# A hybrid trunk layer with expert retrieval: 128 tokens sent ahead of the other 384, dense expert stages cut from 384 to 256 tokens

## Chip, cores and metric

The kernel runs on one core of one Trainium2 chip. The metric is the device time of one execution in microseconds (us), from launch to the last output. All data are float32, and every weight is read from device memory during the execution.

## The reference

```python
def reference(x, p, ...):                     # x: 512 tokens x 1024, one layer
    h = rms_norm(x, mix_norm)
    aq, ak, av, rq, rk, rv, rg, ga, gr = split(h @ w_in)      # 9216 columns
    y_att = sliding_window_gqa(rope(aq), rope(ak), av, sinks) @ w_o_att   # 8 heads of 128, window 128
    yr = group_norm(retention(rope(rq), rope(rk), rv)) * silu(rg)         # 4 heads, keys 256, values 512
    x = x + (sigmoid(ga) * y_att + sigmoid(gr) * (yr @ w_o_ret)) @ w_out
    x = x + peer(rms_norm(x, ffn_norm))
    x = x + sigmoid(rms_norm(x, ple_norm) @ w_ple_gate) * (p @ w_ple_proj)
    return rms_norm(x, final_norm)

def peer(h):                                   # 8 heads, 16384 experts of one neuron
    q = h @ w_peer_query                       # 2048 columns: 8 heads x 2 halves x 128
    s1, s2 = scores of both halves with 128 sub-keys each
    top 16 of s1, top 16 of s2, top 16 of their 256 sums -> 128 experts a token, softmax gates
    act = gelu(h . expert_down[idx]);  return sum(act * gate * expert_up[idx])
```

Retention is computed as one causal product with a decay matrix over all 512 tokens.

## The kernel before, in words

**Layout.** Activations lie transposed: 8 tiles (`KT`) of 128 features, with tokens along the free dimension. Weights come as units of 128 x 1024 floats (512 KB) in the order of `weight_units`, 390 of them, through a ring of 8 slots (`RING`) filled by SyncE's queue. A slot is loaded again when the unit 8 before has been used (`wait_used`).

**Precision.** Every large product is made of three matmuls of the rounded type float32r (`mm3`: high x high, high x low, low x high). ScalarE writes the high part of a unit (`upper`, L550), GpSimd the low part (`lower`, L493). Small products (scores, transposes, the scatter below) are plain float32 matmuls; the profile records each of these as two.

**Stages, in TensorE's order.** All 512 tokens pass each stage together.
1. Projections and mixers (`columns`: weights stationary, 512 tokens moving; `tokens`: 128 tokens stationary, 512 columns moving; retention heads `for i in range(RH)`, then attention heads `for i in range(AH + 4)`, then `woa`, `ga`, `out`).
2. Queries: 16 units `pq`, each followed by `key_scores`. VectorE then finds the top 16 lists (`best`), decodes positions into expert numbers (`rows_and_columns`, `decode`) and makes the gates.
3. Dense experts for the first 384 tokens (`TD`). `down`: 128 units (keys), each 24 passes over `TZ` = 352 tokens, then gelu on ScalarE, results written to `act_scratch`. From turn 8 on (a turn is 8 units) the gates are scattered into dense form: VectorE makes one-hots (`compare`, `times_gate`), TensorE multiplies them (`scatter`, L1185, 96 groups of four), ScalarE stages them, and they are written to `gate_scratch`. `up`: 128 units, each 18 passes of 512 columns over three token tiles; activations and gates are read back by quads of units (`read_back`), multiplied by VectorE (`weigh`) and split in two.
4. The last 128 tokens are sparse: for each of 128 (head, choice) pairs GpSimd gathers one expert row per token (an indirect DMA, 128 rows of 4 KB, called a row here), and VectorE takes the dot product (`dot`, L1335) or adds it scaled (`axpy`, L1743). 32 extra rows serve 32 more tokens, of which `down` leaves out the first part. There are 160 rows down and 128 up, 8 to 10 in flight, and GpSimd issues them between its `lower` operations by the table `FETCH_AT`. 9 rows are left after the last scatter (`NLAST`).
5. The tail: transposes of the sums, the embedding gate (`pp`, `pg`), the last norm.

The order of all work on every engine is written out by hand.

Of the kernel before, what the change touches and what calls it, by code (L numbers as in the profile page):

```python
# [7 lines left out]
F32 = mybir.dt.float32  # L8
# [18 lines left out]

AQ0, AK0, AV0 = 0, AH * ADH, AH * ADH + AKV * ADH
# [9 lines left out]


# [3 lines left out]
def weight_units():  # L43


# [23 lines left out]
UNITS = weight_units()  # L69
NU = len(UNITS)  # L70
UNIT = {k: n for n, k in enumerate(UNITS)}
DN0, UP0 = UNIT[("dn", 0)], UNIT[("up", 0)]
LEAD = 5


def projection_outputs():


    o = []
    for i in range(RH):  # L80
# [20 lines left out]
ASIDE = (("rk", 0), ("rk", 1))  # L101
SLOT = {k: n for n, k in enumerate(k for k in OUT if k not in ASIDE)}
# [13 lines left out]
for _k, _n in OUT.items():  # L116
# [32 lines left out]
U_SLOTS = 8  # L149
V_OWN, V_SLOTS = 6, 10  # L150
PLAIN_HEADS = 4
DOTS_DECODE, DOTS_HEAD = 2, 13
DOTS_EXP, DOTS_SELECT = 5, 5
DOTS_EARLY = (PH - 1) * DOTS_DECODE + (PH - PLAIN_HEADS) * DOTS_HEAD + DOTS_EXP + DOTS_SELECT
DOT_QUADS = ((1, 3, 5, 7, 9, 10, 11, 13, 14, 15),
# [41 lines left out]

# [1696 lines left out]
```

## Time and profile before

| | before |
|---|---|
| median of 3 runs | 1981.96 us (1981.82 to 1984.06) |
| span of the profiled execution | 1979.5 us, so 2.5 us of the median lie around it |
| TensorE busy | 1956.9 us, 99% |
| VectorE / ScalarE / GpSimd busy | 69% / 41% / 62% |
| moved by DMA | 471.9 MB, 238 GB/s over the span |

A busy share is the time in which at least one instruction of the engine was under way. The DMA share is the mean busy share of 16 DMA engines; it is summed over packets, so it can pass 1.00.

### The profile page before, as it was taken

To read this page: it belongs to the slowest core of one execution; us is meant where nothing else is said; L and a number is where in the kernel's file an instruction comes from. 1 tells how busy PE (TensorE), PEld (TensorE's weight loads), DVE (VectorE), ACT (ScalarE), POOL (GpSimd) and SP (SyncE) were. 2 spreads that over 40 slices of the span, in tenths; PEclk is the share of its full clock that TensorE was granted. 3 is DMA by queue.
4 is the path that set the end of the run, shared out by engine and by line. 5 is a ranking of instruction groups with operands and counts; after the bars stand their busy time and mean duration, and the time that the engine had idled before them with its cause. 6 is when DMAs were issued, how large, how long until landed. Compare 5 with 4: busy or idle time off the path is not lost.

```text
span 1979.5 us, 27319 instructions
## 1 busy us (share of the span) xinstructions
PE 1956.9 (99%) x10232; PEld 1724.9 (87%) x10232; DVE 1365.3 (69%) x2287; ACT 806.0 (41%) x1272; POOL 1234.5 (62%) x686
## 2 busy tenths in 40 slices
PE   7999999999999999999999999999999999999998
PEld 6888888888888888999999999999888888888887
DVE  6433333332831489999968888861998999999976
ACT  5222222232553343433346666654333333333352
POOL 5343434352234433899997767766998988888842
PEclk9999999999999999999999999999999999999999
DMA  5222222233223332899997999998999999999931
GB/s 198 86 90 86 91 85 85 87 116 112 80 75 96 96 128 78 333 333 350 366 360 270 386 377 359 372 389 273 363 372 347 377 357 354 375 364 361 358 108 43
DMA packets 171953, 471.93 MB, mean 238 GB/s; under 512 B 13776, under 2 KB 62928, under 8 KB 170064
## 3 DMA queue, kind: packets, MB, share of 16 engines
q1 hardware_dynamic: 58032, 209.04, 30.5%
q0 software_dynamic: 41472, 151.01, 20.5%
q10 hardware_dynamic: 72352, 110.64, 15.6%
q8 instruction: 54, 0.88, 0.2%
q14 instruction: 43, 0.35, 0.0%
HBM read 413.49 MB, written 54.53 MB: 236 GB/s over the span
## 4 chain that ended last, share of the span: by engine, by line
PE 96%; DVE 2%; ACT 1%; DMA 0%; issue 0%; POOL 0%; POOLq 0%; SPq 0%; DVEq 0%; ACTq 0%
PE bank L932 29%; PE bank L934 29%; PE bank L933 29%; PE bank L1185 4%; PE bank L1047 1%; PE bank L1130 1%; PE bank L1115 1%; PE bank L1091 0%; PE bank L1101 0%; DVE bank L1375 0%; DMA xT<-x_cols 0%; PE bank L1016 0%; PE bank L1138 0%; ACT b_hi L594 0%; DVE h_lo L1383 0%; DVE scr L1422 0%
## 5 line engine op out<-in xcount | busy, mean ns | idle before, releaser
L493 POOL TENSOR_TENSOR w_lo<-raw,w_hi 128x1024 fp32r<-128x1024 f32 x390 | 937.3, 2412 | 650.1 <-ACT w_hi L550 646.9
L932 PE MATMUL bank<-h_hi,w_hi 128*128 128x352 f32 (+2 forms) x1560 | 549.1, 352 | 0.0
L934 PE MATMUL bank<-h_hi,w_lo 128*128 128x352 f32 (+2 forms) x1560 | 538.1, 345 | 0.0
L933 PE MATMUL bank<-h_lo,w_hi 128*128 128x352 f32 (+2 forms) x1560 | 537.2, 344 | 0.0
L550 ACT ACTIVATE w_hi<-raw 128x1024 fp32r<-128x1024 f32 x390 | 407.6, 1054 | 309.8 <-DMA raw<-weights 254.0
L933 PEld LDWEIGHTS bank<-h_lo,w_hi 128*128 128x128 f32 x1560 | 294.7, 189 | 19.7
L934 PEld LDWEIGHTS bank<-h_hi,w_lo 128*128 128x128 f32 x1560 | 293.0, 188 | 20.7
L932 PEld LDWEIGHTS bank<-h_hi,w_hi 128*128 128x128 f32 x1560 | 293.8, 188 | 19.5
L1763 DVE TENSOR_TENSOR b_lo<-scr,b_hi 128x384 fp32r<-128x384 f32 x128 | 267.3, 2088 | 46.3 <-ACT b_hi L846 46.1
L932 PE MATMUL bank<-w_hi,b_hi 128*128 128x512 f32 x768 | 298.9, 389 | 0.0
L934 PE MATMUL bank<-w_hi,b_lo 128*128 128x512 f32 x768 | 298.8, 389 | 0.0
L933 PE MATMUL bank<-w_lo,b_hi 128*128 128x512 f32 x768 | 298.8, 389 | 0.0
L932 PEld LDWEIGHTS bank<-w_hi,b_hi 128*128 128x128 f32 x768 | 144.2, 188 | 30.2 <-DVE b_lo L1763 0.5
L933 PEld LDWEIGHTS bank<-w_lo,b_hi 128*128 128x128 f32 x768 | 144.2, 188 | 30.0
L934 PEld LDWEIGHTS bank<-w_hi,b_lo 128*128 128x128 f32 x768 | 144.2, 188 | 29.8
L754 ACT ACTIVATE scr<-bank 128x352 f32<-128x352 f32 x128 | 58.7, 458 | 150.0 <-PE bank L934 149.9
L932 PE MATMUL bank<-b_hi,w_hi 128*128 128x512 f32 x272 | 108.2, 398 | 10.6 <-DVE b_lo L1350 9.2
L846 ACT ACTIVATE b_hi<-scr 128x384 fp32r<-128x384 f32 x128 | 66.7, 521 | 122.9 <-DVE scr L1754 122.5
L932 PE MATMUL bank<-w_hi,h_hi 128*128 128x512 f32 (+1 forms) x288 | 109.7, 381 | 1.1 <-DVE h_lo L1383 1.1
L934 PE MATMUL bank<-w_hi,h_lo 128*128 128x512 f32 (+1 forms) x288 | 108.8, 378 | 0.0
L933 PE MATMUL bank<-w_lo,h_hi 128*128 128x512 f32 (+1 forms) x288 | 108.7, 378 | 0.0
L1335 DVE SCALAR_TENSOR_TENSOR more<-more,bank 128x1024 f32<-128x1024 f32 x80 | 96.9, 1211 | 15.8 <-DMA more<-peer_down,scr 9.1
(227 smaller groups left out, 2705.0 us busy)
## 6 DMA issues: line engine op xcount, KB each, us to landing
raw<-weights SPq DMA_DIRECT2D x390, 512.0 KB, 6.2
act_scratch<-scr ACTq DMA_DIRECT2D x64, 384.0 KB, 7.1
gate_scratch<-scr ACTq DMA_DIRECT2D x12, 2048.0 KB, 13.5
scr<-gate_scratch ACTq DMA_DIRECT2D x22, 768.0 KB, 9.6
scr<-act_scratch ACTq DMA_DIRECT2D x22, 768.0 KB, 14.8
xT<-gate_scratch ACTq DMA_DIRECT2D x10, 768.0 KB, 8.9
xT<-act_scratch ACTq DMA_DIRECT2D x10, 768.0 KB, 14.9
scr<-scr ACTq DMA_DIRECT2D x20, 128.0 KB, 3.9
```

Of the source, the lines that this page charges most:

```text
L493: return nc.gpsimd.tensor_tensor(w_lo[:, s, :], raw[:, s, :], w_hi[:, s, :].bitcast(F32), ALU.subtract)
L550: nc.scalar.activation(w_hi[:, u_mod, :], raw[:, u_mod, :], ACT.Copy).then_inc(hi_done, 1)
L754: nc.scalar.activation(act[:, c % 4, 0:TZ], bank[:, c % 2, 0:TZ], ACT.Gelu_apprx_tanh).then_inc(act_ready, 1)
L846: nc.scalar.activation(b_hi[:, c % 4, 0:TD], wgt[:, c % 2, :], ACT.Copy).then_inc(wgt_hi_ready, 1)
L932: nc.tensor.matmul(out, a_hi, c_hi, start=first, stop=False)
L933: nc.tensor.matmul(out, a_hi, c_lo, start=False, stop=False)
L934: return nc.tensor.matmul(out, a_lo, c_hi, start=False, stop=last)
L1047: ins = nc.tensor.matmul(bank[:, 2 + j, 0:S - P * j], r_k[:, c, P * j:P * j + P], r_q[:, c, P * j:S], start=c == 0, stop=c == 1)
L1115: ins = nc.tensor.matmul(bank[:, 7, P * t:P * t + P], a_v[:, t - 1 + b, P * kv:P * kv + P], a_pT[:, t, b, :], start=b == 0 or t == 0, stop ...
L1185: ins = nc.tensor.matmul(scattered(q)[:, x, :], onehot(q, x, 0).bitcast(F32), gated[q % 4][:, x, :], start=True, stop=True)
L1335: stt(out=row, in0=row, scalar=1.0, in1=h_tok, op0=ALU.mult, op1=ALU.mult, accum_out=to[:, n:n + 1]).then_inc(dot_done, 1)
L1763: tt(b_lo[:, c % 4, 0:TD], wgt[:, c % 2, :], b_hi[:, c % 4, 0:TD].bitcast(F32), ALU.subtract).then_inc(wgt_split, 1)
```

## The change

The 512 tokens are split: `E` = 128 early ones and `L` = 384 late ones.

- **Early pass.** The first 128 tokens go alone through all mixers and queries, in 124 units (29 batches, `BATCHES`) with plain float32 matmuls straight from the loaded weights. Nothing is split, so neither `upper` nor `lower` touches these units. The same 124 weight units are loaded again for the late pass: the list of units grows from 390 to 514.
- **Late pass.** The same stages with 384 tokens in `mm3`. The retention values and decayed scores of this pass are no longer split: `r_s` times `r_v` is a plain float32 product.
- **Sparse tokens.** The early 128 tokens are all sparse (256 rows, down and up), and so are the last 128 (256 rows); the 32 extra rows go. There are 512 rows in all, through 8 slots. 168 of them are used in the late mixers, 88 between the steps of the late top-k, 8 before the scatter, 54 in it, 66 after it (`NLAST`), 128 in `up`.
- **Dense stages.** They hold `T` = 256 tokens. In `down`, even units stay `mm3` over 256 tokens, and odd units are plain float32 over 256 tokens. In `up` every unit is plain float32: 4 matmuls of 512 columns, without `weight_upper` and without the split of `weigh`. The scatter has 64 groups of four instead of 96; ScalarE makes all products of one-hot and gate (`gate_quad`) and VectorE none.
- **New waits.** TensorE waits for `y0_ready` after down turn 6 (`early_sums`: the sums of the early rows are transposed and added to `x0`), and for `y0_added` before the gates are transposed. GpSimd waits in `fetch` for the slot's last use (`row_done`).

```diff
+E = P
+L = S - E
+BATCHES = ([("rk", [("rk", 4 * b + n) for n in range(4)]) for b in range(2)]
+           + [("rq", [("rq", 4 * b + n) for n in range(4)]) for b in range(2)]
+           + [("rv", [("rv", 4 * h + c) for c in range(4)]) for h in range(RH)]
+           + [("rg", [("rg", 4 * h + c) for c in range(4)]) for h in range(RH)]
+           + [("akv", [("ak", 0), ("ak", 1), ("av", 0), ("av", 1)])]
...
+           + [("pq", [("pq", 4 * b + n) for n in range(4)]) for b in range(4)])
-UNITS = weight_units()
+UNITS = EARLY + late_units()
-FIRST_Z = 7
+T = 2 * P
+FIRST_Z = 8
+Y0_TURN = 7
+R_SLOTS = 8
...
+for _m in range(KT):
+    ROWS_AFTER[("woa", _m)] = 3 if _m + 2 < KT else 1
+    ROWS_AFTER[("out", _m)] = 1 + _m % 2
...
+AQ_ROWS = {_i: min(3, max(0, _left - 3 * (_i - 1))) for _i in range(1, AH)}
+MIXER_ROWS = sum(ROWS_AFTER.values()) + sum(AQ_ROWS.values())
+TOPK_EARLY = 2 * NPAIR - MIXER_ROWS
+LIST_ROWS = [min(5, max(0, TOPK_EARLY - (5 * _m + 5 * (_m // 2)))) for _m in range(2 * PH)]
+DOTS_EXP, DOTS_SELECT = 4, 4
+QUAD_ROWS = ((1, 3, 4, 6, 7, 8, 9, 10, 11, 12, 13, 15),) + 3 * ((0, 1, 3, 4, 5, 6, 7, 8, 9, 10, 11, 12, 13, 15),)
+FETCH_LAG, FETCH_FIRST = 7, UNIT[("rg", 0)] + 6
+for _r in range(3 * NPAIR):
+    if _r >= R_SLOTS:
+        _at = max(_at, ROW_USED[_r - R_SLOTS] + FETCH_LAG)
+    while len(FETCH.get(_at, ())) >= (2 if _r < R_SLOTS else 4):
+        _at += 1
+    FETCH.setdefault(min(_at, UP0 - 1), []).append(_r)
...
+            def fetch(r):
+                part, n = divmod(r, NPAIR)
...
+                if r >= R_SLOTS:
+                    pool.wait_ge(row_done, r - R_SLOTS + 1)
+                ids = expert_early if part < 2 else expert_late
+                pool.indirect_dma_start(slots[:, r % R_SLOTS, :], None, up_d if part % 2 else down_d,
+                                        bass.IndirectOffsetOnAxis(ap=ids[:, n:n + 1], axis=0)
+                                        ).then_inc(row_landed[r % R_SLOTS], 16)
+            for u in range(NE, UP0):
...
+                if is_split(u):
+                    lower(u)
+                for r in FETCH.get(u, ()):
+                    fetch(r)
+            for r in range(3 * NPAIR, 4 * NPAIR):
+                fetch(r)
...
+            def e_columns(u, out, rhs, ready=None):
+                wait_landed(pe, u)
+                for k in range(KT):
...
+                    ins = nc.tensor.matmul(out, raw[:, u % RING, k * P:k * P + P], rhs[:, k, :],
+                                           start=k == 0, stop=k == KT - 1)
+                ins.then_inc(e_used, 1)
+            def e_tokens(j, u0, nu, out):
...
+                for n in range(nu):
+                    wait_landed(pe, u0 + n)
+                for k in range(KT):
+                    ins = nc.tensor.matmul(out, e_h[:, k, :], raw[:, s:s + nu, k * P:k * P + P],
+                                           start=k == 0, stop=k == KT - 1)
+                ins.then_inc(e_used, nu)
...
             def down(i, c, halfway=None):
-                    ins = mm3(bank[:, c % 2, 0:TZ], w_hi[:, s, P * k:P * k + P], w_lo[:, s, P * k:P * k + P],
-                              h_hi[:, k, 0:TZ], h_lo[:, k, 0:TZ], k == 0, k == KT - 1)
+                    if c % 2 == 0:
+                        ins = mm3(bank[:, c % 2, 0:T], w_hi[:, s, P * k:P * k + P], w_lo[:, s, P * k:P * k + P],
+                                  h_hi[:, k, 0:T], h_lo[:, k, 0:T], k == 0, k == KT - 1)
+                    else:
+                        ins = nc.tensor.matmul(bank[:, c % 2, 0:T], raw[:, s, P * k:P * k + P], h_whole[:, k, :],
+                                               start=k == 0, stop=k == KT - 1)
...
+            def early_sums():
+                pe.wait_ge(s12_ready, 2 * PH)
+                pe.wait_ge(y0_ready, 1)
...
             down_turn(0)
-            with pe.Fori(1, FIRST_Z) as i:
+            with pe.Fori(1, Y0_TURN) as i:
+                down_turn(i)
+            early_sums()
+            with pe.Fori(Y0_TURN, FIRST_Z) as i:
                 down_turn(i)
...
             def up(i, c):
-                        ins = mm3(bank[:, b, :], b_hi[:, c % 4, a], b_lo[:, c % 4, a],
-                                  w_hi[:, s, 512 * n:512 * n + 512], w_lo[:, s, 512 * n:512 * n + 512], first, last)
+                        ins = nc.tensor.matmul(bank[:, b, :], wgt[:, c % 4, a], raw[:, s, 512 * n:512 * n + 512],
+                                               start=first, stop=last)
...
+            def row():
+                r = done[0]
...
+                ve.wait_ge(row_landed[r % R_SLOTS], 16 * (r // R_SLOTS + 1))
+                if part % 2 == 0:
+                    ins = stt(out=u, in0=u, scalar=1.0, in1=row_bank, op0=ALU.mult, op1=ALU.mult,
+                              accum_out=dots[:, n:n + 1])
+                else:
+                    a = act_sparse[:, n:n + 1]
+                    ve.wait_ge(row_done, r)
...
+                        ins = stt(out=row_bank, in0=u, scalar=a, in1=row_bank, op0=ALU.mult, op1=ALU.add)
+                ins.then_inc(row_done, 1)
...
+            rows(NLAST)
+            assert done[0] == 3 * NPAIR
             def weigh(e):
...
-                ve.wait_ge(wgt_hi_ready, e + 1)
-                tt(b_lo[:, c % 4, 0:TD], wgt[:, c % 2, :], b_hi[:, c % 4, 0:TD].bitcast(F32),
-                   ALU.subtract).then_inc(wgt_split, 1)
```

## Rows read from the trace of the kernel before

**Rows 1.** Waits of TensorE, longest: us in total, times, longest.

```profile
PE bank L932 <- DVE b_lo L1350: 9.2, 1, 9.2
```

**Rows 2.** Stages by windows: length, engines busy (instructions), TensorE clock, DMA share, GB/s.

```profile
9.20:692.20 683.00, 678.84 (x3146) 562.26 (x3147) 274.80 (x437) 231.40 (x343) 265.68 (x111) 1.00 0.30 96
692.20:798.20 106.00, 106.00 (x547) 90.24 (x546) 94.49 (x441) 38.43 (x56) 39.64 (x18) 1.00 0.32 101
798.20:1048.00 249.80, 249.80 (x1556) 249.78 (x1555) 220.30 (x635) 103.43 (x141) 223.43 (x141) 1.00 0.96 349
1048.00:1318.00 270.00, 270.00 (x1928) 270.00 (x1928) 225.94 (x297) 170.58 (x382) 194.74 (x129) 1.00 0.95 362
1318.00:1381.00 63.00, 63.00 (x398) 63.00 (x397) 15.82 (x25) 26.65 (x39) 40.21 (x19) 1.00 0.90 317
1381.00:1903.00 522.00, 521.97 (x2305) 432.06 (x2304) 482.92 (x384) 196.71 (x260) 450.46 (x257) 1.00 0.98 353
1903.00:1979.50 76.50, 67.31 (x363) 57.52 (x361) 50.12 (x71) 34.69 (x53) 17.82 (x9) 0.96 0.15 49
```

**Rows 3.** Timeline of TensorE: start, us, instruction (512- and 256-column passes, retention scores).

```profile
1900.01 0.39 PE L932 MATMUL bank<-w_hi,b_hi 128*128 128x512 f32 x1
...
1903.87 0.40 PE L934 MATMUL bank<-w_hi,b_lo 128*128 128x512 f32 x1
...
1959.26 0.28 PE L933 MATMUL bank<-h_lo,w_hi 128*128 128x256 f32 x1
...
1963.58 0.28 PE L933 MATMUL bank<-h_lo,w_hi 128*128 128x256 f32 x1
...
60.23 4.48 PE L1047 MATMUL bank<-scr 128*128 128x512 f32 x16
64.46 0.48 PE L932 MATMUL bank<-w_hi,h_hi 128*128 128x512 f32 x1
```

**Rows 4.** Chain that ended last, one scatter of four plain float32 matmuls.

```profile
1051.30 0.89 PE bank L1185 x8
```

**Rows 5.** Timeline of VectorE during the queries: start, us.

```profile
719.09 0.88 DVE L1594 MAX8 scr<-scr 128x8 f32<-128x128 f32 x4
...
730.01 0.23 DVE L1647 COPY bank<-scr 128x64 f32<-128x64 f32 x1
...
736.00 0.87 DVE L1594 MAX8 scr<-scr 128x8 f32<-128x128 f32 x4
```

**Rows 6.** Groups of VectorE, 700 to 1050 us: count, busy, mean ns, idle before.

```profile
L1335 DVE SCALAR_TENSOR_TENSOR xT<-xT,bank 128x1024 f32<-128x1024 f32 x39 | 47.2, 1209 | 6.2 <-DMA xT<-peer_down,scr 6.0
...
L1625 DVE TENSOR_TENSOR scr<-bank,small 128x2048 f32<-128x2048 f32 x8 | 18.3, 2291 | 0.3
...
L1633 DVE TENSOR_REDUCE scr<-scr 128x96 f32<-128x1536 f32 x8 | 14.0, 1753 | 0.3
...
L1335 DVE DVE_READ_ACCUMULATOR more<-more,bank 128x1 f32 x38 | 3.1, 83 | 0.0
```

**Rows 7.** Timeline of VectorE in the attention heads, one head.

```profile
517.58 1.23 DVE L1517 SCALAR_TENSOR_TENSOR scr<-bank,scr 128x1024 f32<-128x1024 f32 x1 [1.87 <-issue]
...
524.53 0.68 DVE L1542 TENSOR_TENSOR b_lo<-bank,b_hi 128x512 fp32r<-128x512 f32 x1
527.02 1.22 DVE L1517 SCALAR_TENSOR_TENSOR scr<-bank,scr 128x1024 f32<-128x1024 f32 x1 [1.80 <-issue]
```

**Rows 8.** Shorter windows, columns as in the second group.

```profile
12.00:16.00 4.00, 4.00 (x15) 3.18 (x14) 2.97 (x5) 3.75 (x6) 2.37 (x1) 1.00 1.04 417
...
800.00:1030.00 230.00, 230.00 (x1430) 230.00 (x1429) 203.69 (x615) 90.57 (x122) 213.42 (x135) 1.00 0.98 356
1090.00:1120.00 30.00, 30.00 (x215) 30.00 (x215) 25.83 (x35) 18.07 (x40) 21.03 (x16) 1.00 1.01 403
1400.00:1860.00 460.00, 459.97 (x2030) 380.64 (x2029) 433.95 (x345) 171.37 (x224) 403.13 (x235) 1.00 1.01 362
```

**Rows 9.** DMA issues from 100 to 400 us: KB each, median us to landing.

```profile
raw<-weights SPq DMA_DIRECT2D x48, 512.0 KB, 3.7
```

More of the change, by code:

```diff
@@ new lines @@
+for _k in (("ak", 0), ("ak", 1), ("gr", 0)):
+    ROWS_AFTER[_k] = 2
+for _m in range(KT):
+    ROWS_AFTER[("wor", RH - 1, _m)] = 1
+for _m in range(KT):
+    ROWS_AFTER[("woa", _m)] = 3 if _m + 2 < KT else 1
+    ROWS_AFTER[("out", _m)] = 1 + _m % 2
+for _m in range(RAW_Q):
+    ROWS_AFTER[("pq", _m)] = 2
+for _m in range(2, KT - 2):
+    ROWS_AFTER[("gr", _m)] = 2
+_left = NPAIR - sum(ROWS_AFTER.get(_k, 0) for _k in OUT if OUT[_k] < OUT[("aq", 0)])
+AQ_ROWS = {_i: min(3, max(0, _left - 3 * (_i - 1))) for _i in range(1, AH)}
@@ L532, in _ @@
+            for r in range(3 * NPAIR, 4 * NPAIR):
+                fetch(r)
+            for u in range(PP0, NU):
+                lower(u)
             for k in range(FINAL_DVE, KT):
@@ new lines, in e_add_up, with e_spread @@
+            def e_add_up(r):
+                pe.wait_ge(e_kept, KEPT[("sq0", "sq2")[r]])
+                b = (2, 6)[r]
+                for k in range(KT):
+                    ins = nc.tensor.matmul(bank[:, b, 0:1], e_sq[:, k, :], ones[:, 0:1], start=k == 0, stop=k == KT - 1)
+                ins.then_inc(e_made, 1)
+            def e_spread():
+                pe.wait_ge(e_inv_ready, 1)
+                nc.tensor.matmul(bank[:, 3, 0:E], e_inv[:, 0:1].to_broadcast([P, P]), ident,
+                                 start=True, stop=True).then_inc(e_made, 1)
@@ new lines, in e_token_rows @@
+            def e_token_rows():
+                for k in range(KT):
+                    ins = nc.tensor.transpose(row_bank[:, P * k:P * k + P], e_gained[:, k, :], ident)
+                ins.then_inc(e_made, 1)
+            pe.wait_ge(small_landed, 16)
+            e_batch(0, e_u, ready=(e_gained_ready, 0), after={2: lambda: e_add_up(0)})
+            e_batch(1, e_u, after={1: e_spread, 4: lambda: add_up(0)})
+            e_batch(2, e_u, after={2: lambda: spread(0)})
+            e_batch(3, e_u)
@@ new lines, in _ @@
+            e_wor(FIRST_OF["wor"] + 1)
+            e_att_out()
+            for b in range(2):
+                e_batch(FIRST_OF["ga"] + b, e_h)
+            pe.wait_ge(e_kept, KEPT["att1"])
+            for b in range(2):
+                e_batch(FIRST_OF["woa"] + b, e_att)
+            e_batch(FIRST_OF["out"], e_merged, ready=(e_merged_ready, 0))
+            e_batch(FIRST_OF["out"] + 1, e_merged)
+            e_batch(FIRST_OF["pq"], e_gained, ready=(e_gained_ready, 2), after={2: lambda: e_add_up(1)})
@@ L1062, in _ @@
                 columns(("ak", n), h_hi, h_lo)
-            tokens([("av", t) for t in range(TT)], UNIT[("av", 0)], AKV)
+            tokens([("av", t) for t in range(LT)], UNIT[("av", 0)], AKV)
             transposes(RH - 1, (0, 1))
@@ new lines, in best, with each @@
+            def best(lists, more=0):
+                def each(f, row_after):
+                    together([lambda a=a: f(*a) for a in lists], row_after)
+                each(lambda src, rest, v, p: nc.vector.max(v[:, 0:8], src), more > 0)
+                each(lambda src, rest, v, p: nc.vector.max_index(p[:, 0:8], v[:, 0:8], src), more > 1)
+                each(lambda src, rest, v, p: nc.vector.match_replace(rest, v[:, 0:8], src, LOWEST), more > 2)
+                each(lambda src, rest, v, p: nc.vector.max(v[:, 8:16], rest), more > 3)
+                each(lambda src, rest, v, p: nc.vector.max_index(p[:, 8:16], v[:, 8:16], rest), more > 4)
```

1590 lines of the change are left out of this document (1014 added, 576 removed), and 10 rows, old and new, of tables (DOT_QUADS, FETCH_AT).

## Prediction

> **What bounds the kernel now.** I read the waits of TensorE first, then the stages by windows. TensorE's only long wait is the 9.2 us before its first matmul [rows 1]. After it the engine is busy in every microsecond up to 1903, at full clock [rows 2]. So each stage lasts as long as its matmuls. The reader is to see a second thing in the same windows: from 798 to 1903 us the DMA share is 0.90 to 0.98 at 317 to 362 GB/s, while in the mixers it is 0.30 [rows 2]. The stretch after the mixers is bound by TensorE with DMA close behind it; the mixers have DMA and VectorE (275 of 683 us) to spare.
>
> **Prices of a matmul.** Seventeen 512-column passes take 1900.01 to 1903.87, 0.227 us each; 36 passes of 256 columns take 1959.26 to 1963.58, 0.120 us [rows 3]. That is N/2.4 ns plus 13 ns, so 384 columns cost 0.173 us. Plain float32 is bounded from both sides: the retention scores, 2560 columns, take 60.23 to 64.46, 1.65 ns per column [rows 3]; four scatter matmuls, 512 columns, take 0.89 us, 1.74 ns [rows 4]. I take 1.74 ns for narrow ones (0.222 us for 128 columns) and 1.68 for 512-wide ones (0.86 us), which are nearest to the scores.
>
> **Early pass, added.** 90 units of eight 128-column matmuls: 90 x 1.78 = 160 us. Eight groups of four `rv`/`rg` units, 8 x 0.86 each: 55. The `av` pair 3.5. Small products (16 query scores, retention 4 x 0.86, attention, transposes, sums): 21. Together 240 us. Its start needs `small` and 0.5 MB of `x0` instead of 2 MB: I keep about 10 us. Waits: in `rv`, `rg` and `wor` four slots come free at once, so 2.1 MB must land within 6.9 to 7.1 us; at 417 GB/s, which the weights alone reach [rows 8], that is 5.0 us, plus a lone unit's 3.7 us to landing [rows 9] less its own 1.3 us: 7.4 us, 0.4 us late twelve times. With the hand-overs between chained batches (merged, x, gained) 12 us. Bounds 0 and 50. Late pass starts at 10 + 240 + 12 = 262.
>
> **Late mixers, shrunk.** Before, `pq` starts at 692.2 [rows 2]. My parts give 74 units x 24 x 0.227 = 403, values and gates 174, `av` 11.5, scores 17, split y products 27, transposes 8, attention 8 x 4.0 = 32 and 10 of waits and sums, 683 against 683 measured. With 384 tokens: 74 x 24 x 0.173 = 308; 24 x 24 x 0.227 = 131; 9; 15.5; plain y products 31; 6; attention 27.5: 528 us. New waits: an attention head occupies VectorE for about 7.4 us with 0.3 idle, of a period of 9.4 [rows 7]; at three quarters plus three rows of 1.29 us (1209 + 83 ns [rows 6]) it wants 10.1 us where TensorE wants 7.5. Some 5.5 heads x 2.6 = 14 us. Group norm hidden behind shorter `rq` matmuls 5, the rest 6: 25 us. `pq` starts at 262 + 553 = 815.
>
> **Queries and down, to the select.** TensorE's own work: 16 x (4.16 + 0.67) = 78, then 70 units. An even one is 24 x 0.120 = 2.88, an odd one 2048 columns = 3.47 (3.38 to 3.56): 3.18 mean against 3.83 before. That makes 78 + 222 + 4 = 304 us. VectorE is longer. One head before is two lists and a sum, 719.09 to 736.00, 16.9 us [rows 5], of which 5.5 a list; decoding is 8 us a head by its groups (2.29 twice, 1.75 [rows 6], smaller ones). At 384 tokens I take 12.9 and 6.1. Start after the norm and 8 rows 30 us; 8 heads 103; 8 decodes 49; positions 16; 88 rows x 1.29 = 114; two sums into `x0`, 4 rows, gates: 11. Sum 323 us. In the list part this asks 96 rows' and 67 units' traffic, 93 MB in 225 us, 412 GB/s, against 403 GB/s as the best 30 us [rows 8]: 10 us more. So the gates are ready at 333 and TensorE has waited 29 us, partly at `y0_ready`, partly at `sel_ready`. What is queued behind these waits on TensorE is two down units and the whole scatter, for which ScalarE and VectorE wait in turn. To the first scatter 8 us.
>
> **Scatter.** Before: 270 us for 96 scatters and 48 units. After 32 x (3.18 + 1.78) = 159 us. One turn moves 16.5 MB (8 units, 8 results, 4.2 MB of gates, 13.5 rows) in 39.7 us, 416 GB/s: 164 us at 403. VectorE has 16 compares and 14 rows, 37 us a turn, ScalarE about 35: both hidden, by 3 us. If that cover goes, 3 to 10 us more.
>
> **Rest of down.** Before, 9 rows followed the last scatter; now 66 do. TensorE needs 24 x 3.18 = 76 us; VectorE 66 x 1.29 = 85. DMA must bring 24 units, 58 rows, three quads to read back, and writes 24 results: 49 MB, 122 us at 403 GB/s. GpSimd adds 6: it issues these rows only after the `lower` of late units, three to four per unit, and waits for `row_done` before each; behind that wait stand the next `lower`, and behind it `down`. 128 us, a wait of 52 us for TensorE. Bounds 112 to 145.
>
> **Up.** Four 512-wide matmuls: 3.39 to 3.56 us a unit, 3.46 with start: 443 us against 522. The traffic per unit falls from 1.48 to 1.35 MB (0.52 weights, 0.56 rows, 0.26 read back); less what was fetched ahead it is 161 MB in 443 us, 363 GB/s, and the kernel before holds 362 there without one wait of TensorE [rows 1, 8]. The split of `weigh` (2.1 us of VectorE a unit) and GpSimd's `lower` go at no gain, since TensorE hid them. The tail stays 76.5 us.
>
> **Sum.** 262 + 553 + 333 + 8 + 164 + 128 + 443 + 76.5 = 1967.5 us of span, against 1979.5. With 2.5 us around the span (1981.96 less 1979.5) that is 1970 us. Of the matmuls saved after the mixers, about 170 us, some 90 come back as waits, and the mixers with their early pass cost 123 us more.
>
> **Rival 1, memory holds the rate of before (slower).** From `pq` to the end of `up` the new kernel still moves 394 MB: 272 units 143, 344 rows 180, results and gates written 34, read back 34, x. Before it is 400 MB in 1211 us [rows 2]. If the 362 GB/s of `up` [rows 8] is a ceiling and not TensorE's demand, this takes 1088 us plus 25 in which VectorE holds all: 815 + 1113 + 76.5 + 2.5 = 2007 us. It decides below 371 GB/s, where the total passes 1982. For it: 0.98 share at 356 GB/s [rows 8]. Against it: 403 over 30 us with rows, gates and weights mixed, 417 for weights alone [rows 8]. The Trainium skill ("DMA: Bandwidth & Descriptors", Specifications and Where 436 GB/s comes from) speaks against the change here: it gives about 358 GB/s as a core's share of the memory, and a fabric ceiling of 435. By the first figure the time would be an estimated 2020 us. The 417 GB/s of this trace lies above it; no run here shows it as a limit.
>
> **Rival 2, everything keeps pace (much faster).** The early waits are gone, the select comes at TensorE's own 304, the scatter at 159, the rest of down at VectorE's 85, up at 441. That is 250 + 538 + 304 + 8 + 159 + 85 + 441 + 76.5 + 2.5 = 1864 us, with some row waits 1870 to 1940. It needs 49 MB in 85 us, 580 GB/s; no row is near it, so only its upper part is likely.
>
> **Rival 3, the hand-overs of the early pass (slower).** With 124 units of 1.78 us each batch passes over VectorE and ScalarE before the next. Upper bounds: 50 us early instead of 12, and rows that GpSimd's order makes late in the mixers, 50 instead of 25. 2020 to 2035 us. For it: ScalarE must keep one order over norm, copies and table changes; against it: VectorE was busy 40% of this stage [rows 2].
>
> **How the numbers follow.** A measurement here tells 0.2%, 4 us, from no change. Forecast 0.45, its own range 1945 to 1995: 0.29 faster, 0.07 same, 0.09 slower. Rival 1 0.24 (0.02 same, 0.22 slower), rival 2 0.18, all faster, rival 3 0.13, slower. Faster 0.47, same 0.09, slower 0.44. The range for 8 in 10, from the upper part of rival 2 into rivals 1 and 3: 1905 to 2035.
>
> **What would show it.** Steps of 1.78 us per early unit; `pq` of the late pass at 815; pairs of down units of 6.35 us; two new waits of TensorE, on the early sums and on the gates, together 29 us; DMA at 400 GB/s or more in down, with the last turns stretched to 5.3 us a unit and GpSimd waiting for VectorE's rows; up units of 3.46 us. If up units come at 3.6 or more with DMA at 360, rival 1 holds; if TensorE shows idle time in the early pass beyond 15 us, rival 3.

## The result, and the profile after

The changed kernel takes 2083.8 us (median of 4 runs, 2075.1 to 2090.0), the kernel before 1981.9: 1.051 times as long, 95% interval 1.048 to 1.054. Forecast were 1970 us and a range of 1905 to 2035. The profiled execution took 2086.6 us, with a span of 2084.8.

These are the stages of the changed kernel by windows (columns as in [rows 2]): the early pass, then of the late pass the retention heads, the attention heads, and the gates with both output projections; the queries, down to the early sums, the wait for the gates, the start of the scatter, the scatter, the rest of down with the wait for `up`, `up`, the tail.

```profile
10.80:261.40 250.60, 244.22 (x1730) 208.60 (x1731) 63.46 (x161) 42.82 (x81) 5.31 (x3) 0.99 0.79 282
261.40:687.30 425.90, 387.41 (x1875) 336.90 (x1873) 267.53 (x565) 128.62 (x161) 298.80 (x195) 0.96 0.71 244
687.30:803.80 116.50, 80.20 (x410) 73.61 (x411) 69.76 (x142) 45.46 (x97) 39.69 (x30) 0.83 0.46 152
803.80:908.00 104.20, 99.38 (x560) 99.06 (x559) 69.30 (x77) 37.98 (x55) 79.71 (x50) 0.97 0.70 243
908.00:996.30 88.30, 81.91 (x478) 80.65 (x476) 70.68 (x173) 31.34 (x52) 63.26 (x49) 0.94 0.80 285
996.30:1184.80 188.50, 180.15 (x1120) 167.77 (x1121) 166.01 (x456) 51.86 (x86) 139.42 (x104) 0.98 1.00 390
1184.80:1243.90 59.10, 47.16 (x305) 43.84 (x304) 56.18 (x205) 15.34 (x25) 19.58 (x11) 0.94 0.65 215
1243.90:1256.00 12.10, 11.28 (x58) 10.69 (x58) 12.07 (x15) 3.98 (x11) 6.39 (x5) 0.75 0.61 203
1256.00:1427.50 171.50, 161.14 (x1142) 151.86 (x1143) 130.00 (x165) 133.29 (x363) 85.32 (x68) 0.99 0.95 360
1427.50:1568.40 140.90, 86.42 (x482) 78.84 (x480) 84.16 (x138) 19.80 (x37) 88.97 (x80) 0.81 1.03 407
1568.40:2010.90 442.50, 442.50 (x1025) 195.75 (x1026) 209.99 (x258) 7.43 (x8) 129.15 (x127) 0.99 1.00 375
2010.90:2084.80 73.90, 65.05 (x350) 55.77 (x348) 47.80 (x70) 33.35 (x51) 15.54 (x8) 0.96 0.14 51
```

Laid beside the sum of the prediction, term by term:

| term | forecast | measured | difference |
|---|---|---|---|
| start of the late pass | 262 | 261.4 | -0.6 |
| late mixers | 553 | 646.6 | +93.6 |
| queries and down to the gates | 333 | 335.9 | +2.9 |
| to the first scatter | 8 | 12.1 | +4.1 |
| scatter | 164 | 171.5 | +7.5 |
| rest of down | 128 | 140.9 | +12.9 |
| `up` | 443 | 442.5 | -0.5 |
| tail, and around the span | 79 | 75.7 | -3.3 |
| together | 1970 | 2086.6 | +116.6 |

One term holds four fifths of the error. In the late mixers TensorE is busy for 387 + 80 + 99 = 567 of 646.6 us, and its granted clock is 0.83 of full on average in the attention. The waits of TensorE over the whole execution, longest first, as in [rows 1]:

```profile
PE bank L1184 <- POOL w_lo L650: 43.7, 11, 8.4
PE bank L1672 <- DVE scr L2378: 28.1, 1, 28.1
PE bank L1540 <- DVE hb L2174: 18.5, 7, 5.8
PE bank L1510 <- ACT scr L963: 16.7, 7, 6.3
PE bank L1649 <- DVE scr L2336: 12.0, 1, 12.0
```

The reader is to see who ends them. L650 is GpSimd's `lower`: L1184 is the first matmul of a unit that needs its low part. L1540 and L1510 are attention: the transposes wait for VectorE's `b_lo` (L2174), the products of probabilities and values for ScalarE's copy (L963). L1672 is the start of `up`, L1649 the wait for the gates. Before, there was one wait of 9.2 us [rows 1].

In the attention, this is one head, timeline of GpSimd, VectorE, ScalarE and TensorE (start, us, instruction; the idle time before it and what ended it in brackets; L664 is the gather of a row, L1772 its dot product, L700 ScalarE's high part of a unit):

```profile
721.53 1.04 ACT L700 ACTIVATE w_hi<-raw 128x1024 fp32r<-128x1024 f32 x1
...
722.65 2.40 POOL L650 TENSOR_TENSOR w_lo<-raw,w_hi 128x1024 fp32r<-128x1024 f32 x1 [8.59 <-ACT w_hi L700]
...
725.20 0.95 POOL L664 DMA_INDIRECT slots<-peer_down,scr  x1
...
731.28 1.22 DVE L1772 SCALAR_TENSOR_TENSOR slots<-slots,bank 128x1024 f32<-128x1024 f32 x1 [6.57 <-DMA slots<-peer_down,scr]
...
732.43 0.55 DVE L2174 TENSOR_TENSOR hb<-bank,hb 128x384 fp32r<-128x384 f32 x1
...
733.04 1.33 PE L1540 MATMUL bank<-small,scr 128*128 128x128 f32 x5 [5.82 <-DVE hb L2174]
```

Read it as a chain. GpSimd's lower part waits 8.59 us for ScalarE, the gathers stand behind the lower part, VectorE stands still for 6.57 us until the row lands, and `b_lo` comes behind the row in VectorE's order. TensorE's transposes then start at 733.04, after 5.8 us of waiting.

In the retention heads GpSimd works in bursts. Within one it has no pause (timeline of GpSimd, after a set of slots has come free):

```profile
487.12 2.41 POOL L650 TENSOR_TENSOR w_lo<-raw,w_hi 128x1024 fp32r<-128x1024 f32 x1
489.69 0.95 POOL L664 DMA_INDIRECT slots<-peer_down,scr  x1 [0.16 <-issue]
490.95 0.93 POOL L664 DMA_INDIRECT slots<-peer_down,scr  x1 [0.30 <-issue]
491.90 2.37 POOL L650 TENSOR_TENSOR w_lo<-raw,w_hi 128x1024 fp32r<-128x1024 f32 x1
```

A lower part and two gathers take 491.90 - 487.12 = 4.78 us, and TensorE uses a unit of 384 tokens in 4.17. A gather costs GpSimd 1.2 to 1.26 us; the kernel before gathered none in the mixers. After the value and gate units, which give four slots back at once, GpSimd waits up to 13.2 us for the high part of the next unit, and then is behind again. So over the retention heads it is busy for 299 of 426 us, and is late all the same.

### The profile page after: what moved, and what is told of

Its sections match the earlier page's. It is cut to its first block, busy times and chain, and to the rows that moved or that the text cites. A ratio compares the mean times of both kernels' runs of the same rounds, so it can differ in the third digit from the quotient of the medians.

```text
span 2084.8 us, 25711 instructions
## 1 busy us (share of the span) xinstructions
PE 1886.8 (91%) x9521; PEld 1503.3 (72%) x9521; DVE 1247.7 (60%) x2421; ACT 553.4 (27%) x1024; POOL 971.3 (47%) x726
## 4 chain that ended last, share of the span: by engine, by line
PE 55%; DVE 14%; DMA 12%; POOL 10%; issue 5%; ACT 3%; SPq 0%; ACTq 0%; POOLq 0%; DVEq 0%
PE bank L1672 21%; DMA slots<-peer_down,scr 8%; PE bank L1184 6%; PE bank L1186 6%; PE bank L1185 6%; PE bank L1269 6%; POOL w_lo L650 5%; POOL slots L664 5%; DVE slots L1772 2%; PE bank L1290 2%; PE bank L1600 2%; DVE bank L1780 2%; DMA raw<-weights 2%; DMA slots<-peer_up,scr 1%; PE bank L1344 1%
## 5 line engine op out<-in xcount | busy, mean ns | idle before, releaser
L650 POOL TENSOR_TENSOR w_lo<-raw,w_hi 128x1024 fp32r<-128x1024 f32 x198 | 472.3, 2392 | 637.9 <-ACT w_hi L700 635.8
L1184 PE MATMUL bank<-hb,w_hi 128*128 128x384 f32 (+2 forms) x1320 | 450.2, 341 | 55.0 <-POOL w_lo L650 28.0
L1672 PE MATMUL bank<-raw,scr 128*128 128x512 f32 x1024 | 442.6, 595 | 28.1 <-DVE scr L2378 28.1
L1185 PE MATMUL bank<-hb,w_hi 128*128 128x384 f32 (+2 forms) x1320 | 431.5, 327 | 0.0
L1186 PE MATMUL bank<-hb,w_lo 128*128 128x384 f32 (+2 forms) x1320 | 431.2, 327 | 0.0
L1772 DVE SCALAR_TENSOR_TENSOR slots<-slots,bank 128x1024 f32<-128x1024 f32 x256 | 308.8, 1218 | 173.0 <-DMA slots<-peer_down,scr 165.4
L664 POOL DMA_INDIRECT slots<-peer_up,scr x256 | 244.2, 954 | 343.8 <-DVE bank L1780 291.6
L1672 PEld LDWEIGHTS bank<-raw,scr 128*128 128x128 f32 x1024 | 195.6, 191 | 274.7 <-issue 274.7
L700 ACT ACTIVATE w_hi<-raw 128x1024 fp32r<-128x1024 f32 x198 | 205.3, 1053 | 559.1 <-DMA raw<-weights 548.8
L1780 DVE SCALAR_TENSOR_TENSOR bank<-slots,scr,bank 128x1024 f32<-128x1024 f32 x254 | 325.7, 1282 | 33.7 <-DMA slots<-peer_up,scr 29.6
L1184 PEld LDWEIGHTS bank<-hb,w_hi 128*128 128x128 f32 x1320 | 262.4, 199 | 66.1 <-POOL w_lo L650 29.5
L664 POOL DMA_INDIRECT slots<-peer_down,scr x256 | 243.3, 950 | 108.4 <-issue 79.7
L1185 PEld LDWEIGHTS bank<-hb,w_hi 128*128 128x128 f32 x1320 | 262.4, 199 | 4.8 <-issue 1.0
L1186 PEld LDWEIGHTS bank<-hb,w_lo 128*128 128x128 f32 x1320 | 261.4, 198 | 2.9
L1021 ACT ACTIVATE scr<-bank 128x256 f32<-128x256 f32 x128 | 48.4, 379 | 231.1 <-PE bank L1186 136.8
L1184 PE MATMUL bank<-w_hi,hb 128*128 128x512 f32 (+1 forms) x216 | 86.0, 398 | 19.3 <-POOL w_lo L650 15.7
## 6 DMA issues: line engine op xcount, KB each, us to landing
gate_scratch<-scr ACTq DMA_DIRECT2D x8, 2048.0 KB, 8.8
x_all<-x_scratch ACTq DMA_DIRECT2D x1, 2048.0 KB, 17.4
```

The costliest lines, as they stand in the source:

```text
L650: nc.gpsimd.tensor_tensor(w_lo[:, s, :], raw[:, s, :], w_hi[:, s, :].bitcast(F32), ALU.subtract).then_inc(lo_done, 1)
L664: pool.indirect_dma_start(slots[:, r % R_SLOTS, :], None, up_d if part % 2 else down_d, bass.IndirectOffsetOnAxis(ap=ids[:, n:n + 1], axis ...
L700: nc.scalar.activation(w_hi[:, u_mod, :], raw[:, u_mod, :], ACT.Copy).then_inc(hi_done, 1)
L1184: nc.tensor.matmul(out, a_hi, c_hi, start=first, stop=False)
L1185: nc.tensor.matmul(out, a_hi, c_lo, start=False, stop=False)
L1186: return nc.tensor.matmul(out, a_lo, c_hi, start=False, stop=last)
```

## The experiments

Theory 1: the gathers, put between GpSimd's lower parts, hold TensorE. Theory 2: VectorE is full with the rows. Theory 3: the hand-overs of a pass with 384 tokens are too long with or without rows. The table gives each run by the same boundaries (us, from the first and the last matmuls of each part, in one profiled execution of each kernel); "late mixers" is the sum of the three parts before it, "rest" the rest of down with the wait for `up`. In runs 1, 2, 3, 8, 10, 13 and 15 a part of the rows' work is left out; the others do all of it.

| kernel | retention | attention | gates, out | late mixers | scatter | rest | median |
|---|---|---|---|---|---|---|---|
| changed | 425.9 | 116.5 | 104.2 | 646.6 | 171.5 | 140.9 | 2083.8 |
| 1 no rows in mixers | 375.9 | 105.2 | 95.6 | 576.7 | 170.5 | 141.2 | 2008.8 |
| 2 rows on VectorE only | 378.9 | 109.4 | 100.5 | 588.8 | 174.6 | 141.0 | 2026.0 |
| 3 rows gathered only | 420.6 | 109.3 | 104.2 | 634.1 | 174.6 | 141.1 | 2067.0 |
| 4 lag 5 | 411.8 | 111.3 | 105.0 | 628.1 | 160.2 | 137.1 | 2048.0 |
| 5 copy first | 423.9 | 129.6 | 104.1 | 657.6 | 169.8 | 141.4 | 2097.6 |
| 6 lag 3 | 465.7 | 111.8 | 104.8 | 682.3 | 160.4 | 132.8 | 2094.8 |
| 7 copy first, lag 4 | 423.5 | 110.2 | 104.8 | 638.5 | 157.6 | 135.2 | 2057.2 |
| 8 copy first, no rows | 376.0 | 103.7 | 95.6 | 575.3 | 174.0 | 141.4 | 2006.3 |
| 9 out at 7 | 423.7 | 118.0 | 101.0 | 642.7 | 170.2 | 141.3 | 2081.1 |
| 10 out at 7, no rows | 374.4 | 75.6 | 93.5 | 543.5 | 174.2 | 141.1 | 1975.8 |
| 11 out at 7, lags 5 and 4 | 405.9 | 87.9 | 102.8 | 596.6 | 159.1 | 133.9 | 2015.8 |
| 12 rows before lower | 413.2 | 93.8 | 102.9 | 609.9 | 158.7 | 134.2 | 2026.7 |
| 13 stand-in for gathers | 412.3 | 110.1 | 103.6 | 626.0 | 173.3 | 140.8 | 2063.5 |
| 14 two gathers a unit | 412.8 | 85.9 | 99.7 | 598.4 | 161.2 | 133.7 | 2018.6 |
| 15 out at 7, VectorE only | 378.9 | 84.8 | 96.9 | 560.6 | 170.7 | 140.9 | 1999.0 |

**Runs 1 to 3: the rows taken apart.**

```diff
             def fetch(r):
+                if r < MIXER_ROWS:
+                    return
...
             def row():
+                src = x_all[:, 0:D] if r < MIXER_ROWS else u
...
+                if r < MIXER_ROWS and r != NPAIR:
+                    ins = ts(dots[:, n:n + 1] if part == 0 else misc[:, 156:157], u[:, 0:1], 1.0, None, ALU.mult)
```

Runs 1 and 2 have the first two parts of this, and do not wait for these rows to land; runs 1 and 3 have the last (in run 1 with a column of a constant for `u`). `r != NPAIR` leaves one row in at full width.

> The changed kernel without the work of the 168 rows of the late mixers: none is gathered, and VectorE does a one-column operation in the place of each (a full one for the first up row). So the late mixers stand alone. In the changed kernel they last 650 us (261.4 to 911.5) where 553 was forecast: 528 of TensorE's own work, 25 of waits. Theory 1 (rows gathered by GpSimd between its lower parts hold up TensorE): about 560 us, total about 1990. Theory 2 (VectorE is full with the rows): the same here, 560. Theory 3 (the chain of hand-overs of a mixer with 384 tokens is too long whether or not there are rows; the attention heads above all): 620 us or more, total 2050 or more. The fourth step, rows, then does not matter much.

> The changed kernel with the 168 rows of the late mixers not gathered, but worked on by VectorE at full width (from a tile that lies in memory already). VectorE has its whole load, GpSimd has only the lower parts, and nothing lands late. Theory 1 (GpSimd's order): late mixers 570 to 585 us, total near 2005. Theory 2 (VectorE full): 625 to 650 us, total 2060 to 2084. Theory 3: 620 or more in this one and in the one without rows.

> The changed kernel with the 168 rows of the late mixers gathered as before, but VectorE, having waited for each, only does a one-column operation on it (a full one for the first up row). Its load is that without rows; GpSimd's and the transfers are whole. Theory 1 (GpSimd's order): late mixers 620 to 650 us, total 2055 to 2084. Theory 2 (VectorE full): 565 to 580 us, total near 2000.

Measured: 2008.8 us without rows (1.0134 times before, 1.0114 to 1.0155), 2026.0 with VectorE's part alone, 2067.0 with the gathers alone (its two runs 15 us apart). The retention heads by windows, of the kernel without rows, with VectorE's part, and with the gathers, a fence each:

```profile
261.00:636.90 375.90, 373.45 (x1875) 327.74 (x1874) 154.12 (x460) 128.33 (x160) 187.14 (x79) 1.00 0.34 119
```

```profile
259.70:638.60 378.90, 374.04 (x1875) 327.76 (x1874) 263.69 (x566) 128.40 (x160) 187.02 (x79) 1.00 0.34 118
```

```profile
261.20:681.90 420.70, 385.54 (x1876) 335.23 (x1874) 160.20 (x457) 128.63 (x161) 299.68 (x195) 0.96 0.72 248
```

VectorE's rows, with VectorE 264 of 379 us busy, cost 3 us here. The gathers, with GpSimd 300 us busy and the DMA share at 0.72 for 0.34, cost 45; these two are taken apart in run 13. Over all late mixers VectorE's rows are worth 12 us (576.7 to 588.8) and the gathers 58 (588.8 to 646.6). Theory 1 has most of it, theory 2 falls. But without any row the mixers still take 577 us, not 553 and not the 560 of theory 1, and 105 of them are attention, in which TensorE is busy for 75 at a clock of 0.90: theory 3 has a share of its own.

**Run 4: earlier gathers.** `FETCH_LAG` is the number of units between the use of a row and the gather of the next one into its slot.

```diff
-FETCH_LAG, FETCH_FIRST = 7, UNIT[("rg", 0)] + 6
+FETCH_LAG, FETCH_FIRST = 5, UNIT[("rg", 0)] + 6
```

> FETCH_LAG 5 instead of 7: each row that follows another in its slot is asked for two units earlier in GpSimd's order, nothing else changes, no work is left out. If rows that land late are what holds VectorE and, through it, TensorE (in the attention heads, where the rows of a unit are gathered after the lower part that waits for ScalarE in the same unit, and in the rest of down): attention 30 us shorter, rest of down some 10, total 2040 to 2050. If GpSimd's own rate (2.4 us a lower part plus 1.25 a row) is the limit, only the attention gains: 2055. If VectorE is full, or if GpSimd now waits for slots with the lower parts queued behind: 2080 or more.

Measured: 2048.0 us, 1.033 times before (1.031 to 1.035), 36 us less than the changed kernel. The total was as expected and the places were not: 14 us came in the retention heads, where VectorE's wait for rows fell from 48.4 to 10.5 us, 5 in the attention, 11 in the scatter, 4 in the rest.

**Runs 5, 7 and 8: ScalarE's copy first.**

```diff
             for i in range(AH + 4):
+                if 0 <= i - 4 < AH:
+                    h = i - 4
...
+                    sc.wait_ge(pv_done, h + 1)
+                    nc.scalar.activation(b_hi[:, h, :], late(7), ACT.Copy).then_inc(b_hi_ready, 1)
                 if i < AH:
                     to_tile(("aq", i), ACT.Copy)
                     swap_halves(AKV + i, q_swap)
-                if 0 <= i - 4 < AH:
...
```

> The changed kernel with one order turned round on ScalarE in the attention heads: the copy of the finished head into its high part comes before the copy of the next query and its swap, and not behind them. No work is left out. Without rows the attention still took 105 us (TensorE alone 77) in a loop of 13.8 us a head: query done, ScalarE copies it and issues two swaps (1.8 us), then the head's high part, VectorE's low part, and only then TensorE's transposes, which wait for the bank. Theory 3 (this hand-over is a part of the loss of its own): attention 116 to 95 us, total 2062. If the rows that land late set these heads anyway (4 to 6.6 us of VectorE's wait before a row in a head): 112 to 116 us, total 2078 to 2084.

> ScalarE's copy first, and no work for the 168 rows of the late mixers (none gathered; a one-column operation in the place of each). Without rows alone it was 2009 us, the late mixers 577, the attention 105. Theory 3: attention 80 to 88, total 1985 to 1990, so that late mixers come to 555, which is the forecast of 553 for them with rows. If something else holds the heads: 2000 or more.

> Both edits: ScalarE's copy first, and FETCH_LAG 4. If hand-over and late rows are separate causes, their gains add: 36 of the lag and 20 of the copy give 2028; with lag 4 as with 5. If they cover each other: 2040 to 2048. A lag of 4 that is already too short for GpSimd would show 2045 or more with its waits for slots in the retention heads.

Measured: 2097.6, 2006.3 and 2057.2 us. The gain of theory 3 came in none of them. Run 5 was slower than both of its cases; run 8 came out in its last case, something else holds the heads; run 7 in its last too, with 39.5 us of GpSimd's waits for slots in the retention heads. Without rows TensorE's wait for `b_lo` went (9.2 us in run 1), but the one for ScalarE's copy of the probabilities (L963 above) stayed, 20.9 us for 18.9, and so did the loop, 13.6 us a head for 13.8: 103.7 us for 105.2. With rows it cost 13 us: ScalarE now waits for TensorE before it makes the next unit's high part, so GpSimd's lower part is later, and so are the gathers behind it. VectorE's waits for rows in the attention rose from 22.3 to 36.8 us.

**Run 6: the gathers earlier still.** The edit of run 4 with a lag of 3.

> FETCH_LAG 3 instead of 7 (5 gave 2048 us). GpSimd asks for a row as soon as three units after the use of the row before in its slot, in its own order, which runs about four units ahead of TensorE: so it now waits for VectorE with lower parts behind it. If lateness of rows is all that the lag governs: 2035 to 2045. If GpSimd's waits for slots hold the lower parts back: slower than with 5, 2055 to 2075, with TensorE's waits for lower parts in the mixers above the 44 us of the changed kernel.

Measured: 2094.8 us, slower as the second case said, but past its 2075. The waits of GpSimd for VectorE's slots and of TensorE for lower parts, in the retention heads of this kernel:

```profile
POOL slots L664 <- DVE slots L1772: 118.1, 27, 29.4
PE bank L1184 <- POOL w_lo L650: 68.1, 8, 10.4
```

In the changed kernel these two were 9.6 and 15.7 us. VectorE hardly waits for rows now (2.4 us), and it is worse: a gather that comes too early stops every lower part behind it.

**Runs 9 and 10: the products later.** This edit stands on top of that of run 5.

```diff
-                columns(key, h_hi, h_lo, at_tile={3: lambda: att_out(i - 4)} if 0 <= i - 4 < AH else {})
+                columns(key, h_hi, h_lo, at_tile={7: lambda: att_out(i - 4)} if 0 <= i - 4 < AH else {})
```

> ScalarE's copy first, as in the run at 2098 us, and the products of probabilities and values of a finished head put before the eighth tile of the next query unit instead of the fourth. Nothing is left out. Without rows the copy first left the attention at 104 us: each head takes 13.6 us, and the loop is scores, VectorE's maximum (3.0 us), ScalarE's exponentials and copy (2.7), then these products, behind which five tiles and the next scores stand. With one tile behind them, 3 to 4 us a head should go. If that loop is what binds the heads with rows too: attention 130 to 100 us, total 2060. If the rows (asked for behind the lower part, which waits for ScalarE) bind them: 120 or more, total above 2085.

> The same two edits, without the work of the 168 rows of the late mixers (none gathered, a one-column operation in the place of each). If the loop over scores, exponentials and products is what is left of the attention (104 us against 77 of TensorE's work): 75 to 82 us, total 1978 to 1984, with TensorE's clock in that stretch back at 1.0 from 0.9. If not: 100 and 2004.

Measured: 2081.1 us with rows, 1975.8 without (0.9973 times before, 0.9962 to 0.9983). The late mixers of the second, by windows:

```profile
263.30:637.70 374.40, 371.97 (x1876) 326.25 (x1875) 154.30 (x460) 128.43 (x160) 187.31 (x79) 1.00 0.35 119
637.70:713.30 75.60, 66.29 (x423) 62.01 (x422) 49.01 (x119) 44.97 (x97) 22.28 (x10) 1.00 0.26 79
713.30:806.80 93.50, 92.10 (x532) 91.66 (x531) 32.30 (x74) 36.09 (x52) 52.10 (x23) 1.00 0.38 124
```

TensorE is busy for 372 + 66 + 92 = 530 us, where the prediction had 528. So TensorE's own work was priced right, and a head now takes 8.6 us instead of 13.6. With rows the same two edits do nothing for the attention (116.5 to 118.0, where 100 or 120 and more were expected): there VectorE waits 32.0 us for rows, and TensorE 32.7 us for the `b_lo` behind them.

**Runs 11 and 12: both together.** Run 11 is run 9 with `FETCH_LAG` 5 for the mixers' rows and 4 behind them. Run 12 also turns GpSimd's order round in the attention:

```diff
+                early = UNIT[("aq", 3)] <= u < UNIT[("woa", 0)] + 4
+                for r in FETCH.get(u, ()) if early else ():
+                    fetch(r)
                 if is_split(u):
                     lower(u)
-                for r in FETCH.get(u, ()):
+                for r in FETCH.get(u, ()) if not early else ():
                     fetch(r)
```

> The two edits in the attention, and FETCH_LAG 5 for the rows of the mixers and 4 for those behind them. Nothing is left out. The lags are worth 36 us (measured at 5) and 4 more by the stages behind the mixers at 4; the attention's edits 16 to 25 if loop and rows are separate. Total 2020 to 2030; 2045 if only the lags count.

> As the run before it in this call, and in the attention heads GpSimd asks for the rows of a unit before the lower part of that unit, not behind it. The lower part waits 7 to 11 us for ScalarE there. If it is this order that makes the rows late, the attention falls to 85 us with rows, total 2005 to 2015. If VectorE is full in the heads (8 us of its own and 3.9 of rows in a head): the attention stays at 95 or more, total 2020 to 2030.

Measured: 2015.8 us (1.018 times before, 1.016 to 1.020) and 2026.7. In the late mixers the attention's edits alone took 4 us and the lag alone 18.5; together 50.0. They are not two gains that add but two chains side by side, of which the longer one sets the head. Run 12 did not bring the 2005 to 2015 for which it was made: GpSimd then waits 28.1 us for slots in the attention, with the lower parts behind it (1.8 in run 11), and the attention takes 93.8 us instead of 87.9. Its retention heads, which the edit does not touch, are 7 us longer too (413.2 for 405.9): so much the profiled executions of two kernels can differ, and that of run 11 was the fastest of its four.

**Run 13: what of a gather costs.**

```diff
+STAND_IN = 512
...
+                if r < MIXER_ROWS:
...
+                    nc.gpsimd.tensor_tensor(slots[:, 6 + r % 2, 0:STAND_IN], small[:, 0:STAND_IN],
+                                            small[:, 0:STAND_IN], ALU.add).then_inc(spent, 1)
+                    return
```

VectorE works on these rows as in run 2, in four slots instead of eight.

> As the run with the rows on VectorE only (2026 us: 168 rows worked on at full width from a tile in memory, none gathered), and GpSimd adds two tiles of 512 columns, about 1.2 us, wherever it would issue one of these 168 gathers. So GpSimd's time is spent and nothing is moved; it also does not wait for a slot. If GpSimd's time between the lower parts is what a gather costs: 2060 to 2084 us, the retention heads 415 us or more. If it is the traffic of the rows or their late landing: 2026 to 2032, retention heads 379.

Measured: 2063.5 us, against 2026.0 without the stand-ins. Their group on GpSimd, over the late mixers (count, busy, mean ns):

```profile
L662 POOL TENSOR_TENSOR slots<-small 128x512 f32<-128x512 f32 x163 | 172.5, 1082 | 0.0
```

And the retention heads by windows:

```profile
263.40:675.60 412.20, 383.34 (x1874) 333.90 (x1873) 291.32 (x565) 128.16 (x161) 302.79 (x193) 0.97 0.32 108
```

With no byte moved for these rows (DMA share 0.32, 0.71 in the changed kernel) the retention heads rise from 379 to 412 us (426 in the changed kernel). So with GpSimd's time spent and nothing moved, at 1.08 us each, 37 of the 58 us of the gathers come back; a gather takes 1.2 to 1.26. Some of the 37 are likely the stand-in's own; how many was not measured. It is a tensor operation, and some of VectorE's stood still beside it: one small product with the gates took 12.55 us while GpSimd worked back to back, 0.29 in run 2 and 2.20 in the changed kernel, and VectorE is busy for 291 us in these heads instead of 264. TensorE's longest wait there, 8.2 us, ended with VectorE. The other 21 us belong to the longer gather, the traffic and the waits for late rows; these three were not told apart.

**Runs 14 and 15.** Run 14 is run 11 with at most two gathers in a unit for the mixers' rows (up to four before); run 15 is run 9 with the mixers' rows on VectorE only.

> As the best version so far (ScalarE's copy first, products at the eighth tile, lags 5 and 4: 2016 us), and at most two gathers in one unit for the rows of the mixers, where up to four stood. Nothing is left out. If the bursts are what makes the lower parts late (TensorE waits 2.5 to 5 us at the first value and gate unit of a retention head): retention 406 to 395 us, total 2005. If it is GpSimd's whole load (2.4 us a lower part, 1.2 to 1.25 a gather, 30 rows in a head of 20 units): the same within 5 us, or slower where rows now come later, 2016 to 2030.

> The attention's two edits, and the 168 rows of the mixers on VectorE at full width without a gather. Without gathers and without the attention's edits it was 2026; with the edits and no rows 1976, retention 374, attention 76. If VectorE's share is small and separate: retention 378, attention 78 to 80, total 1985 to 1992. If VectorE becomes the bound of the shorter attention heads (8 us of its own and 3.9 of rows against 9.4 of TensorE in a head): attention 90, total 2000.

Measured: 2018.6 us, within 3 of run 11, so spreading the gathers gains nothing. That rules out the bursts and fits GpSimd's whole load, without showing it. Run 15 took 1999.0 us, between its two cases but near the second, with the attention at 84.8 us: in the shorter heads VectorE's rows are worth 9 us (4 in the longer ones).

No version with all its work done beats the kernel before. The best, run 11, is 34 us slower. Run 10, which leaves the rows of the mixers out altogether, is 5 us faster.

## Why the prediction was wrong

**The step that failed** is "Late mixers, shrunk", and in it the "New waits" of 25 us. TensorE's own 528 us were right (530 in run 10). In place of 25 us the late mixers lost 117 (646.6 less 530), and run by run:

- 33 us are the attention's order (run 1 less run 10). The prediction took VectorE's load, 10.1 us a head against 7.5, and so 14 us in all (its own terms, 7.4 x 0.75 + 3 x 1.29, give 9.4 and not 10.1, so 11). The loop is another one: scores, maximum, exponentials, copy, and then the products, with five of eight tiles of the next query behind them. It is 13.8 us long without any row (13.6 in run 8). The diff moves these products from the end of the step to the fourth tile, and the low part of the finished head ahead of the transposes, which share a bank with it; the prediction costed neither.
- 58 us are the gathers (run 2 less the changed kernel). The prediction gave them no time on GpSimd in the mixers. It named GpSimd's order in rival 3 and, at 6 us, in "Rest of down", as a matter of late rows. The price stood in groups of GpSimd in the kernel before that the prediction did not read (count, busy, mean ns, idle before), the lower part and a gather:

```profile
L493 POOL TENSOR_TENSOR w_lo<-raw,w_hi 128x1024 fp32r<-128x1024 f32 x390 | 937.3, 2412 | 650.1 <-ACT w_hi L550 646.9
...
L517 POOL DMA_INDIRECT xT<-peer_down,scr x80 | 76.2, 952 | 18.6 <-issue 13.9 <-DVE scr L1632 2.2 <-DVE more L1335 0.3
```

  With 30 rows and 16 units in a retention head (not 20, as an expectation had it) GpSimd needs 16 x 2.4 + 30 x 1.25 = 76 us, where TensorE needs 79.0 (from the scores of one head to those of the next, runs 1 and 10). It can't use all of the 79, since the weights of four units come at once after a wait; in the changed kernel the last two heads take 87.1 and 95.9 us.
- 12 us are VectorE's rows (run 1 to run 2), for which 14 were allowed.
- The remaining 14 are waits that were there in run 10 too, within the 25 forecast.

These shares hold in this order only. With the attention mended first, the gathers are worth 82 us (run 9 less run 15), VectorE's rows 17 (run 15 less run 10) and the attention's edits 4 (the changed kernel less run 9). The sum is the same.

Part of each is the clock. In the changed kernel the granted clock was 0.96 in the retention heads, 0.83 in the attention, between waits of 0.5 to 6.4 us, and 0.97 behind it. TensorE was busy 567 us in the three, for the work that takes 530 at full clock in run 10. So 37 of the 117 us, whichever wait they followed, are TensorE working at a lower clock, which the prediction did not count; it priced every wait at its own length. In the other 80 TensorE stood still.

**Rival 3** had one of the right places and too small a price: "rows that GpSimd's order makes late in the mixers, 50 instead of 25", and hand-overs of the early pass at 50 instead of 12. Against the 50, the new waits of the mixers were 117, of which the gathers are 58 and the attention's order, which no rival names, 33. The early hand-overs did not happen: the early pass ended at 261.4 for 262 forecast, at 1.81 us a unit (10.88 us for 6) for 1.78.

**Rival 1 is refuted.** `up` ran at 3.46 us a unit, as forecast, and moved 375 GB/s for 442 us; the rest of down moved 407 GB/s for 141 us. The 362 GB/s of before [rows 8] were TensorE's demand. The Trainium skill ("DMA: Bandwidth & Descriptors", Specifications) gives 358 GB/s as a core's share of the memory; the trace does not agree, with 407 over 141 us on this one core. The same page (Bandwidth) ties that figure to both cores of a memory domain streaming, and no run here had a second core. **Rival 2** failed where it let the stages keep pace: the late mixers took 646.6 us for its 538, and the rest of down, at 407 GB/s, 140.9 for its 85.

**Right, with small misses.** Queries and down to the gates: 335.9 for 333. Of the 29 us of waits forecast, 12.0 stood at the gates, 8.6 in front of units of down, and none at `y0_ready`. TensorE was busy 6.43 us for a pair of down units (180.2 over 28) for 6.35. The scatter's +7.5 came from late rows: with lags 5 and 4 it takes 159.1 us, which is TensorE's 159. The rest of down was memory's, as forecast (share 1.03 throughout), and 12.9 us longer, since it moved 57 MB (407 x 140.9) and not 49; a shorter lag, which brings rows forward, gave 7 of these back. The 6 us for GpSimd's waits are not seen there: it waited 1.2 us for slots, and VectorE 59.9 us for rows. Two slips changed nothing that matters: by the prediction's own terms the matmuls saved after the mixers were 1211 - (304 + 159 + 76 + 443) = 229 us, not 170, and 93 MB at 403 GB/s take 6 us more than the 225, not 10.

## What to carry to other kernels

Work that is put into the spare time of one engine also costs time on the engine that issues it: price a gather on the engine that issues it, and compare that engine's load with the consumer's pace in the shortest period, not over the stage. When a tile shrinks, write out the loop of hand-overs for one iteration (here scores, maximum, exponentials, copy, products) and compare its length with the new matmul time: here 13.8 us against 8.6. And two chains that are about equally long hide each other: mending one alone showed 4 us, the other 18.5, both 50.

## What the runs showed of the hardware

- A gather of 128 rows occupies GpSimd for 0.93 to 0.98 us plus 0.16 to 0.30 us before the next. The Trainium skill ("DMA: Bandwidth & Descriptors", SWDGE vs HWDGE vs iDMA) says that descriptors of DMAs issued from GpSimd are written by its own software; the trace agrees in so far as gathers and lower parts stand one behind the other in GpSimd's timeline, 4.78 us for one lower part and two gathers.
- In the attention of the changed kernel TensorE waited once or twice a head, 0.5 to 6.4 us each time, and the granted clock was 0.83, a mean of stretches at the full and at the half level. Over the late mixers its busy time for the same work was 567 us for 530 at full clock.
- While GpSimd ran tensor operations back to back (575.2 to 586.9 us of run 13), one VectorE operation on 128 x 128 that takes 0.29 us in run 2 took 12.55 us (574.5 to 587.1).
- Memory gave 407 GB/s over 141 us with weights, rows, gates and results mixed.
